# Sixteen weight buffers and four high buffers in the expert loop, blocks numbered in TensorE's order of use, loop turns of 16 experts

## The reference

```python
u = rmsnorm(x, ffn_norm_g)                        # 512 x 1024
s = sigmoid(u @ w_router)                         # 64 experts, 8 chosen per token
y = sum over the 8 chosen e of w[e] * swiglu(u, w_exp_up[e], w_exp_down[e])
x = x + y + swiglu(u, w_shared_up, w_shared_down)
# swiglu(t, up, down): gate, value = split(t @ up); (silu(gate) * value) @ down
# w_exp_up[e]: 1024 x 512, w_exp_down[e]: 256 x 1024
```

## Time and profile before

| what | value |
|---|---|
| median of 3 runs | 1233.05 us (1232.86 to 1239.28) |
| profiled execution | 1232.66 us, span 1230.4 us |
| TensorE busy | 1135.6 us (92%) |
| VectorE busy | 902.0 us (73%) |
| ScalarE busy | 724.5 us (59%) |
| GpSimd busy | 259.0 us (21%) |
| moved by DMA | 285.58 MB, 232 GB/s on average |
| the expert loop | from about 575 to 1210 us |

### The profile page before, as it was taken

One profiled execution on the slowest core, in us unless ns is written; L12 is line 12 of the kernel. 1 busy time (PEld: TensorE's weight loads), 2 busy tenths in 40 slices (PEclk: granted clock), 3 DMA queues, 4 the chain that ended last, 5 costly groups with the idle time before them and its releaser, 6 DMA issues.

```text
span 1230.4 us, 16284 instructions
## 1 busy us (share of the span) xinstructions
PE 1135.6 (92%) x5707; PEld 856.4 (70%) x5707; DVE 902.0 (73%) x1133; ACT 724.5 (59%) x926; POOL 259.0 (21%) x145
## 2 busy tenths in 40 slices
PE   4999998988999899998999999999999999999993
PEld 3699997766777688774666666666666666666662
DVE  4575468445433586688998899999889888989881
ACT  7543342343333422513887887888778788888771
POOL 1000000000000000001233434334444434434431
PEclk9999998999999999999999999999999999999997
DMA  6413232221212233267899999999999999999972
GB/s 210 137 52 103 86 95 69 69 69 34 68 35 68 95 111 132 86 261 282 310 360 366 355 370 371 361 367 371 369 364 376 362 372 370 374 372 369 359 270 33
DMA packets 74495, 285.58 MB, mean 232 GB/s; under 512 B 10868, under 2 KB 33416, under 8 KB 49620
## 3 DMA queue, kind: packets, MB, share of 16 engines
q1 hardware_dynamic: 59716, 251.16, 54.3%
q0 software_dynamic: 14736, 33.87, 11.5%
HBM read 272.39 MB, written 29.38 MB: 245 GB/s over the span
## 4 chain that ended last, share of the span: by engine, by line
PE 53%; DMA 24%; DVE 10%; issue 6%; ACT 6%; SPq 0%; DVEq 0%; POOL 0%; ACTq 0%; POOLq 0%
PE bank L1452 43%; DMA arena<-in_w_exp_up_dram 15%; DMA out_dram<-arena 8%; ACT high L554 3%; DVE low L1356 2%; PE bank L1620 2%; PE bank L1647 2%; DVE gatheredT L1363 1%; PE bank L1531 1%; ACT arena L554 1%; PE bank L1833 1%; PE bank L1778 1%; PE bank L1632 1%; DMA arena<-in_x_dram 1%; ACT front_split L554 1%
## 5 line engine op out<-in xcount | busy, mean ns | idle before, releaser
L1356 DVE TENSOR_TENSOR low<-arena,high 128x2048 fp32r<-128x2048 f32 x192 | 436.5, 2287 | 53.6 <-ACT high L554 52.7
L554 ACT ACTIVATE high<-arena 128x2048 fp32r<-128x2048 f32 x192 | 365.2, 1918 | 30.3 <-DMA arena<-in_w_exp_up_dram 30.2
L1452 PE MATMUL bank<-high,gatheredT 128*96 128x512 f32 x1024 | 324.6, 398 | 22.7 <-DVE gatheredT L1363 22.0
L516 POOL DMA_INDIRECT arena<-u_rows,arena x64 | 136.9, 2139 | 591.1 <-DVE arena L1351 562.4
L1452 PEld LDWEIGHTS bank<-high,gatheredT 128*96 128x96 f32 x1024 | 160.2, 161 | 95.9 <-issue 26.8
L1452 PE MATMUL bank<-low,gatheredT 128*96 128x512 f32 x512 | 201.9, 394 | 0.0
L524 POOL DMA_INDIRECT out_dram<-arena x64 | 116.0, 1812 | 365.2 <-ACT arena L554 250.4
L1452 PE MATMUL bank<-high,hidT 128*96 128x512 f32 x512 | 164.7, 403 | 1.5 <-ACT arena L554 1.5
L554 ACT ACTIVATE arena<-bank 96x512 f32<-96x512 f32 (+4 forms) x217 | 107.9, 533 | 65.8 <-PE bank L1452 28.6
L1452 PE MATMUL bank<-hT_high,front_split 128*128 128x512 f32 x448 | 144.3, 404 | 0.8 <-DVE hT_low L892 0.8
L1452 PEld LDWEIGHTS bank<-low,gatheredT 128*96 128x96 f32 x512 | 82.6, 161 | 36.1
(11 more groups left out here) (253 smaller groups left out, 1402.9 us busy)
## 6 DMA issues: line engine op xcount, KB each, us to landing
arena<-in_w_exp_up_dram SPq DMA_DIRECT2D x128, 1024.0 KB, 22.9
arena<-in_w_exp_down_dram SPq DMA_DIRECT2D x64, 1024.0 KB, 19.2
arena<-in_w_in_dram SPq DMA_DIRECT2D x14, 1024.0 KB, 5.4
arena<-in_w_in_dram SPq DMA_DIRECT2D x10, 768.0 KB, 4.5
arena<-in_w_branches_dram SPq DMA_DIRECT2D x4, 1024.0 KB, 4.9
arena<-in_w_out_dram SPq DMA_DIRECT2D x4, 1024.0 KB, 5.0
arena<-in_x_dram SPq DMA_DIRECT2D x4, 512.0 KB, 5.3
arena<-in_w_mem_kv_dram SPq DMA_DIRECT2D x2, 1024.0 KB, 5.0
```

The costliest lines, as they stand in the source:

```text
L516: pool.indirect_dma_start(gathered[0:ROWS, e % 2, :], None, u_dram, bass.IndirectOffsetOnAxis(ap=index[0:ROWS, e:e + 1], axis=0), bounds_c ...
L554: return nc.scalar.activation(o, i, ACT.Copy, **kw)
L1356: v.tensor_tensor(low_part[q % SLOTS], raw[q % SLOTS], high_part[q % HIGHS].bitcast(F32), ALU.subtract).then_inc(low_done, 1)
L1452: ins = mm(bank, left[a], right[b], start=first and q == 0, stop=last and q == 2)
```

## The change

- `SLOTS` goes from 12 to 16, `HIGHS` from 6 to 4. The two high buffers given up become raw slots (10, 11), and two more slots (12, 13) lie where the router kept its small arrays; these move to buffers that are free by then (`place`, `w_high`, `w_low`, `token_of`).
- Blocks are numbered in TensorE's order of use: `up_at(n, j)` is 3n-1+j and `down_at(n)` 3n+4 within a turn (the first up has 0 and 1, the last down the last number). SP loads in this order, each load waits for exactly the block 16 before it. The first fill waits for what frees each slot: `set_done` for 10 and 11, `folded` for 12 and 13, the stored rows for 14 and 15. The four row stores are issued after block 11 (rows 0 and 1) and after block 13 (rows 2 and 3).
- ACT waits before each high copy from the fifth on until TensorE has used the block 4 before it. In an expert, ACT and DVE split both up blocks of n+2 first and the down of n+1 last; before, the down of n+1 and one up first, the other up last.
- `TURN` goes from 4 to 16: 16 experts unrolled, a loop of two passes with 16 in its body, 16 unrolled. The constant table that deals tokens to DMA engines keeps its 4 under the name `DEAL`.
- In the second and later passes over the experts (only when an expert has more than 96 tokens) SP waits for the new index first; in this input's run the text speaks of the first pass alone.

```diff
-TURN = 4
+DEAL = 4
+TURN = 16
 BLOCKS = 3
-SLOTS, HIGHS = 12, 6
-LEAD = 5
+SLOTS, HIGHS = 16, 4
+ROUNDS = BLOCKS * TURN // SLOTS
...
+def up_at(n, j, first=False):
+    return j if first and n == 0 else BLOCKS * n - 1 + j
+
+
+def down_at(n, last=False):
+    return BLOCKS * n + (2 if last and n == TURN - 1 else 4)
...
-        slot_at = [ring_at + 2048 * n for n in (2, 3, 4, 5, 0, 1)] + [gates_at + 2048 * n for n in (0, 1, 4, 5)] + [x_at, x_at + 2048]
+        slot_at = ([ring_at + 2048 * n for n in (2, 3, 4, 5, 0, 1)] + [gates_at + 2048 * n for n in (0, 1, 4, 5, 2, 3)]
+                   + [ib_at, ib_at + 2048, x_at, x_at + 2048])
...
-                     enumerate((ka_at, ka_at + 2048, hT_at, hT_at + 2048, gates_at + 4096, gates_at + 6144))]
+                     enumerate((ka_at, ka_at + 2048, hT_at, hT_at + 2048))]
...
+            def load(src, k, u):
+                s = k % SLOTS
+                if not isinstance(u, int) or k >= SLOTS:
+                    sp.wait_ge(block_used, u + (k - SLOTS + 1))
                 elif s < 4:
                     sp.wait_ge(x1_done, 2 * NT)
                 elif s < 6:
                     sp.wait_ge(front_low, S0 + s - 3)
                 elif s < 10:
                     sp.wait_ge(s_up, NT)
+                elif s < 12:
+                    sp.wait_ge(set_done, 1)
+                elif s < 14:
+                    sp.wait_ge(folded, 1)
                 else:
-                    sp.wait_ge(out_stored, 16 * NT)
+                    sp.wait_ge(out_stored[s - 14], 16 * NT // 2)
+                sp.dma_start(raw[s].rearrange("p k n -> p (k n)"), src).then_inc(raw_in[s], 16)
+
+            def store_rows(k, u):
+                if isinstance(u, int) and k in (11, 13):
+                    for t in (k - 11, k - 10):
+                        sp.wait_ge(out_ready, t + 1)
+                        sp.dma_start(out[0, t * P:(t + 1) * P, :], x_tok[:, t, :]).then_inc(out_stored[t // 2], 16)
+
+            def load_turn(e, n, u, first=False):
+                for j in range(2):
+                    load(up_src[:, e, j, :], up_at(n, j, first), u)
+                    store_rows(up_at(n, j, first), u)
+                if not first or n:
+                    load(dn_src[:, e - 1, :], down_at(n - 1), u)
+                    store_rows(down_at(n - 1), u)
...
+            def high(k, u, round0):
+                if isinstance(u, int) and u + k < HIGHS:
+                    act.wait_ge(s_up, NT)
+                else:
+                    act.wait_ge(block_used, u + (k - HIGHS + 1))
+                act.wait_ge(raw_in[k % SLOTS], round0 * 16 + 16 * (k // SLOTS + 1))
+                copy(high_part[k % HIGHS], raw[k % SLOTS]).then_inc(high_done, 1)
...
+                ups, downs = not last or n + 2 < TURN, not last or n + 1 < TURN
                 act.wait_ge(hidT_done, m + 1)
                 copy(hidT[:, n % 2, 0, :], ps[3][:, 0:2 * ROWS]).then_inc(hidT_high, 1)
                 if not start:
-                    result(n + 1, m - 1, u + 2)
-                for j in range(min(blocks, 2)):
-                    high(q + j, u + (LEAD + j), round0)
+                    result(n + 1, m - 1, u + (down_at(n - 1) + 1))
+                if ups:
+                    high(up_at(n + 2, 0), u, round0)
+                    high(up_at(n + 2, 1), u, round0)
...
+                if downs:
+                    gate_tanh_of(n + 1, m + 1, u + (up_at(n + 1, 1) + 1))
+                if ups:
                     high_tokens(n + 2, m + 2)
-                if blocks > 2:
-                    high(q + 2, u + (LEAD + 2), round0)
+                if downs:
+                    high(down_at(n + 1, last), u, round0)
```

More of the change, by code:

```diff
@@ L470, in _, with load_pass @@
+            def load_pass(u0):
+                for n in range(TURN):
+                    load_turn(n, n, u0, True)
+                with sp.Fori(1, E // TURN) as g:
+                    for n in range(TURN):
+                        load_turn(g * TURN + n, n, u0 + g * (BLOCKS * TURN))
+                load(dn_src[:, E - 1, :], BLOCKS * TURN - 1, u0 + BLOCKS * (E - TURN))
+            load_pass(0)
             sp.wait_ge(routed, 1)
@@ L789, in shared @@
                     elif t == 2:
-                        high(1, 1, 0)
-            def high(q, u, round0):
-                if isinstance(u, int) and u < HIGHS:
-                    act.wait_ge(*((s_up, NT) if u < 4 else (set_done, 1)))
-                act.wait_ge(raw_in[q % SLOTS], round0 * 16 + 16 * (q // SLOTS + 1))
-                copy(high_part[q % HIGHS], raw[q % SLOTS]).then_inc(high_done, 1)
+                        high(1, 0, 0)
+            def high(k, u, round0):
[5 more added lines that the diff above has]
+                copy(high_part[k % HIGHS], raw[k % SLOTS]).then_inc(high_done, 1)
             def high_tokens(n, m):
@@ L823, in expert @@
             def expert(n, m, u, round0, start=False, last=False):
-                q, blocks = BLOCKS * n + LEAD, ahead(n, last)
+                ups, downs = not last or n + 2 < TURN, not last or n + 1 < TURN
                 act.wait_ge(hidT_done, m + 1)
@@ L1232, in shared @@
                 read_deal(0)
-                low(1, 1)
+                low(1, 0)
                 take_down(2)
```

163 lines of the change are left out of this document (68 added, 95 removed).

## The result

The changed kernel is slower, not faster: 1254.38 us (median of 4 runs, 1239.56 to 1256.57) against 1233.2 us in the same job. The recorded ratio, estimated from all executions of both, is 1.0139, with a 95% interval of 1.009 to 1.0188; the two medians by themselves give 1.017. The forecast of 1225.5 us, with its range to 1235, is wrong by 29 us and in the sign. The profiled execution took 1255.38 us, its span is 1253.6 us.

The account below looks back on a forecast made before the run. Engines, then DMA, were taken to bound the expert loop. The later of the DMA bound (1197.6 us) and engine bound (1199.7) put the last transposes 7.1 us earlier: 1232.66 - 7.1 = 1225.6, stated as 1225.5 us, range 1218 to 1235.

Parts of the forecast that it names:

- The views it began with: Expert loop: engines pace it at 9.62 us an expert to about expert 28, then the DMA at 9.97 us.
- (a): First fill, four more buffers: early loads fill the DMA's hole, gaining 9.2 us on its side, ends 6 and 12.2.
- the 12.2 us: DMA time read as unused from 565 to 597 us, where the DMA share is 0.63 against a full 1.02.
- (b): Row stores moved behind blocks 10 to 13: costs nothing, as the first scatter comes 20 us later.
- (c): Loop start: first gather meets a full DMA, lands in 8.9 to 10.1 us; loop starts 3.6 to 4.8 later, taken 4.2.
- (d): New order of loads and splits: nothing in steady state, 0.3 us off the first interval of 10.42 us.
- (e): Four high buffers: second high copy waits 0.5 us longer; its 9.48 us loop is under the 9.62 pace, so nothing.
- Rival D: Slower: the high-buffer loop is longer than read, gain gone at 9.81 us an expert; 1238 to 1244.5 us, chance 0.09.
- (f): Turns of 16: longer loop bodies, same instructions, fewer jumps; zero cost, a few us as upper end.
- the sum: Last expert's transposes at the later of two bounds, DMA 1197.6 and engines 1199.7 us: 7.1 us earlier than before.
- rival C: Little or no gain: loop-end jump costs, more late gathers, or buffers fill late; 1229 to 1235 us, chance 0.25.
- the 4.3 us for late gathers: Engines' bound, expert loop: between one and two more late gathers, 1.5 x 2.9 us.

Follow-up runs that it names:

- s12_t4: Changed kernel with 12 slots in place of 16 and turns of 4 in place of 16, new load order and four high buffers kept: 1234.11 us, ratio 1.0002.
- a_two_chains: Changed kernel with odd experts' results scattered into a second, unread table, each scatter-add waiting for the one two before: 1226.12 us, ratio 0.9936.
- b_t16: Kernel before with turns of 16 experts in place of 4 and nothing else: 1240.83 us, ratio 1.0055.
- b_two_chains: Kernel before with odd experts' results scattered into a second, unread table, each scatter-add waiting for the one two before: 1228.93 us, ratio 0.9966.
- a_one_input: Changed kernel with VectorE's two-input subtraction in the weight split replaced by a one-input multiply: 1253.0 us, ratio 1.0149.

## Why the prediction was wrong

**The views it began with** are right as far as they go: two paces, the DMA's behind the engines'. But the trace of before had GpSimd's 20 waits for a landing, 114.7 us, and 8% of the chain that ended last. I passed them by, since GpSimd was busy 21% of the time. A serial chain isn't seen in a busy share.

**(a)** held: the hole is filled, waits for weights are gone. The earlier trace rows were read a little wrong there: SP's last two first-fill loads go at 577.7 us, and the pair at 580.46 is two loads, the second at 583.3; the 12.2 us don't rest on it. **(b)** held: the first scatter-add was released by ScalarE's copy and not by the stores. **(c)** had the mechanism and a size that was too small. The first token transposes came at 578.67 us, released by the gather, where 579 was forecast, but the hidden transposes 6.45 us late and not 4.2:

```profile
578.67 1.51 PE L1846 MATMUL bank<-arena 96*128 96x96 f32 x8 [7.14 <-DMA arena<-u_rows,arena]
```

The first two gathers, as the earlier trace rows, landed in 11.6 us, where 10.1 was the upper end:

```profile
arena<-u_rows,arena POOLq DMA_INDIRECT x2, 11.6
```

That the transposes still started 578.67 - 574.76 = 3.9 us late, within the 3.6 to 4.8, is luck: the first gather was issued at 567.09 us, 2.4 us earlier than before. The other 2.5 us came behind it. While TensorE stood for 7.14 us, its granted clock fell (columns as in the earlier trace rows):

```profile
570.00:575.00 5.00, 1.53 (x4) 0.38 (x2) 1.23 (x2) 0.00 (x0) 0.60 (x1) 1.00 1.00 379
575.00:580.00 5.00, 1.33 (x8) 1.25 (x8) 0.00 (x0) 0.00 (x0) 0.00 (x0) 0.58 1.01 318
580.00:585.00 5.00, 3.36 (x10) 2.13 (x9) 3.10 (x3) 4.47 (x4) 0.96 (x1) 0.50 1.02 420
```

0.50 is the level of 1.2 GHz; the eight transposes took 1.51 us where they took 0.88. A term for the clock was missing. **(d)** held: s12_t4 has 1.0002. **(e)** held: 3.0 us of waits, and the engines' pace is 9.59 in a_two_chains. Rival D is out. (Its limit of 9.81 us is 607.8 / 62 = 9.80; nothing hangs on it.)

**(f) is the step that failed**, together with a bound that the sum did not have. "Turns of 16: longer loop bodies, the same instructions. [...] Zero, with a few us as the upper end." I looked at the jump, which happens less often in long turns, and not at the code that streams in: 48 experts of straight or first-time code in place of 12, 37 blocks in place of 24. b_t16 prices the longer turn at 1.0055 on the kernel before, some 7 us where the sum had zero; with the new order it is from 1.0002 to 1.0116. That it costs by the code's blocks is the best reading, and not shown. The Trainium skill's "Runtime: NRT & Kernel Launch", section "Instruction fetch mechanics", has both halves: an instruction memory of 2048 instructions for TensorE, which agrees with the second pass of the 16-expert body running without a block (none from 912 to 1094 us), and code refilled in blocks of 16 KB, which it calls mostly hidden. I used its rule on the jump for rival C. No run here shows a jump that costs. That the fetching is hidden agrees with a_two_chains, where 38 blocks are fetched and the pace is 9.59 us; it doesn't agree with the links of a chain that has 0.1 us of slack, which were 0.6 us longer beside a block.

**The sum** took the later of two bounds. There were three: DMA, engines, and the chain at 9.5 us a link if nothing touches it. With the third one taken away a_two_chains gives what was forecast, 1226.12 us for 1225.5 and 1199.83 for 1199.7 us. The agreement is closer than it deserves: the loop started there at 592.55 and not 588.9, and the 4.3 us for late gathers did not come. But the missing bound accounts for the whole miss, whatever it is that tips the chain. The late gathers in "TensorE waits there for the gather" were most likely the chain's mark, which I took for a random event at 2.9 us each: the interval of expert 8, 13.21 us before, is 9.72 in b_two_chains.

Rival C named late gathers and the loop's length, and allowed 1231.5. The size was beyond it because on a chain the cost isn't added per event: a link that is late moves all behind it, and 33 in a row were 0.72 us over the pace.

## What to carry to other kernels

List every serial chain, above all accumulating DMAs that wait for each other, and compare its link with the pace you expect after the change, not the one you have. A bound that is taken away may have been the only slack that such a chain had; ask then what small thing (code, an issue held by another engine) is as large as what is left. If a loop's body is unrolled further, don't put it at zero for having fewer jumps: look at the code that streams in, and measure that line of the change by itself.

## What the hardware showed that I had not expected

- GpSimd's issue of a scatter-add is held by VectorE's subtraction of two SBUF inputs that is under way as it starts: 1.44 us free, up to 3.5 us held, and its end lies 1.32 us after the operation's end. In a_one_input an operation with one input holds it as well, up to 3.1 us, and there most ends lie 0.08 to 0.12 us after the operation's.
- Half the columns make an indirect scatter-add's issue no cheaper: 1.42 us free for 2 KB a row, 1.44 for 4 KB (held ones included, 2.29 and 2.13 in the mean).
- Turns of 16 in place of 4, with 14 more 16 KB blocks of code in 286 MB, went with 0.55% more time (b_t16), though the bytes are one in a thousand.
- TensorE's granted clock fell to half during a wait of 7.14 us for one gather, and the transposes behind it took 1.51 in place of 0.88 us.
